# Turned down product, first layer's second norm on VectorE, and layer two's first weights asked for after the gathers

## The reference

```python
def moe(x, w_router, router_bias, w_gate, w_up, w_down):
    t = x.reshape(B * S, D)                     # D = 1024
    combine = route(t, w_router, router_bias)   # two experts per token, weighted
    h = silu(einsum('td,edf->tef', t, w_gate)) * einsum('td,edf->tef', t, w_up)   # f = 512
    y = einsum('tef,efd->td', h * combine[:, :, None], w_down)

for i in range(DEPTH):                          # 2 layers
    mix = attention(x) if i % 2 == 0 else pool_mix(x)
    x = layer_norm(ALPHA * x + mix, ln1_g[i], ln1_b[i])
    x = layer_norm(ALPHA * x + moe(x, ...), ln2_g[i], ln2_b[i])
```

## Time and profile before

| | |
|---|---|
| median of 3 runs | 1211.73 us (1211.29 to 1215.57) |
| profiled execution, its own time | 1213.42 us |
| its span | 1211.7 us |
| mean granted TensorE clock | 0.932 |
| PE busy | 1054.5 us (87%) |
| DVE busy | 370.1 us (31%) |
| ACT busy | 194.0 us (16%) |
| POOL busy | 111.2 us (9%) |
| DMA | 296.04 MB, mean 244 GB/s |
| chain that ended last | PE 83%, DVE 7%, DMA 4% |

### The profile page before, as it was taken

How to read it: one execution, slowest core, us unless ns; L and a number is a source line. 1 busy time by engine, 2 the same in 40 slices (tenths; PEclk the granted TensorE clock), 3 DMA queues, 4 the chain that set the end, 5 groups by cost and what they waited for, 6 DMA issues and landing times.

```text
span 1211.7 us, 28356 instructions
## 1 busy us (share of the span) xinstructions
PE 1054.5 (87%) x11923; PEld 740.8 (61%) x11923; DVE 370.1 (31%) x798; ACT 194.0 (16%) x428; POOL 111.2 (9%) x184
## 2 busy tenths in 40 slices
PE   7899999899899932999999999178189999999985
PEld 6677777544444322677677668067067776776752
DVE  1334444322433251111111111497511111111117
ACT  1234444400222112000000000131020000000000
POOL 0001001030033103000000000321300000000012
PEclk9999999899999965999999999677589999999997
DMA  9324335230023097999999999606359999999915
GB/s 342 146 86 133 106 112 178 82 79 1 1 78 92 26 392 274 350 384 392 395 385 394 397 389 392 215 3 246 141 200 387 386 395 391 387 400 389 377 51 201
DMA packets 80864, 296.04 MB, mean 244 GB/s; under 512 B 10184, under 2 KB 41168, under 8 KB 72495
## 3 DMA queue, kind: packets, MB, share of 16 engines
q1 hardware_dynamic: 53351, 247.50, 54.5%
q10 hardware_dynamic: 19712, 26.75, 6.5%
q0 software_dynamic: 7760, 21.24, 5.1%
HBM read 255.80 MB, written 40.11 MB: 244 GB/s over the span
## 4 chain that ended last, share of the span: by engine, by line
PE 83%; DVE 7%; DMA 4%; POOL 2%; issue 2%; ACT 2%; ACTq 0%; SPq 0%; POOLq 0%; DVEq 0%
PE PS L896 19%; PE PS L874 15%; PE PS L884 14%; PE PS L801 5%; PE PS L573 4%; PE PS L738 4%; PE PS L620 3%; PE PS L636 3%; PE PS L761 2%; PE PS L529 2%; PE PS L629 2%; PE PS L719 2%; PE PS L551 2%; POOL expert_rows L1036 2%; PE PS L806 1%
## 5 line engine op out<-in xcount | busy, mean ns | idle before, releaser
L896 PE MATMUL PS<-ring,arena 128*96 128x512 f32 x512 | 227.4, 597 | 0.0
L874 PE MATMUL PS<-arena,ring 128*64 128x96 f32 x4096 | 180.5, 250 | 53.5 <-DVE arena L1649 53.5
L874 PEld LDWEIGHTS PS<-arena,ring 128*64 128x64 f32 x4096 | 174.4, 140 | 77.4 <-issue 77.4
L884 PE MATMUL PS<-arena,ring 128*64 128x96 f32 x4096 | 174.4, 246 | 0.0
L884 PEld LDWEIGHTS PS<-arena,ring 128*64 128x64 f32 x4096 | 170.9, 137 | 0.0
L896 PEld LDWEIGHTS PS<-ring,arena 128*96 128x96 f32 x512 | 80.8, 163 | 123.0 <-issue 119.2
L1649 DVE STREAM_TRANSPOSE arena<-arena 128x768 uint32<-128x768 uint32 x34 | 54.2, 1593 | 206.7 <-ACT arena L1227 176.6
L1669 DVE COPY arena<-PS 96x512 f32<-96x512 f32 x32 | 22.0, 687 | 218.0 <-PE PS L896 218.0
L1231 ACT ACTIVATE arena<-PS 96x512 f32<-96x512 f32 x32 | 19.0, 593 | 379.3 <-PE PS L896 379.3
L801 PE MATMUL PS<-ring,arena 128*128 128x512 f32 x128 | 55.7, 594 | 0.7 <-issue 0.7
L1002 POOL DMA_DIRECT2D ring<-cache_krope x64 | 34.6, 541 | 141.3 <-issue 141.3
(11 more groups left out here) (245 smaller groups left out, 1061.2 us busy)
## 6 DMA issues: line engine op xcount, KB each, us to landing
ring<-w_gate SPq DMA_DIRECT2D x32, 2048.0 KB, 15.2
ring<-w_up SPq DMA_DIRECT2D x32, 2048.0 KB, 15.9
ring<-w_down SPq DMA_DIRECT2D x32, 2048.0 KB, 16.3
arena<-expert_rows ACTq DMA_DIRECT2D x144, 96.0 KB, 9.6
expert_out<-arena ACTq DMA_DIRECT2D x32, 384.0 KB, 8.3
expert_rows<-ring SPq DMA_DIRECT2D x6, 1920.0 KB, 10.1
ring<-cache_ckv SPq DMA_DIRECT2D x64, 128.0 KB, 2.1
ring<-w_o SPq DMA_DIRECT2D x1, 4096.0 KB, 19.3
```

The lines of the kernel that those rows point to most:

```text
L874: last = nc.tensor.matmul(bank(s, KF, CAP)[at:at + 64, f, :], wg[w][:, k, P * f + at:P * f + at + 64], xeT[s][:, k, :], start=(k == 0), st ...
L884: last = nc.tensor.matmul(out[at:at + 64, :], wu[w][:, k, P * f + at:P * f + at + 64], xeT[s][:, k, :], start=(k == 0), stop=(k == KD - 1))
L896: last = nc.tensor.matmul(bank(4 + hf)[0:CAP, :], h[s][:, f, :], wd[w][:, f, 512 * hf:512 * (hf + 1)], start=(f == 0), stop=(f == KF - 1))
```

## The change

The down product is turned: w_down becomes the stationary side in chunks of 64 columns and `h` streams, as in gate and up. Its result comes out transposed (`yT`, features on the partitions). ACT and DVE copy the two halves of `yT` out of PSUM, and PE transposes it back (`turn_back`) after the first quarter of the next tile's gate product. Then the rows are copied and stored, one tile later than before. The last tile's is turned back behind the loop.

The second norm of layer one is done by DVE alone, with the sequence of the first norm (`norm`); ACT gives only the deviation. GpSimd issues the gathers alone.

SP asks for `pool_scale` and `state_pool` first, waits for all five gathers, and then asks for layer two's first expert.

```diff
@@ SP
-                    load_expert(1, 0, 1, (S[0]["gate_ps"][0], nh), (S[0]["up_ps"][0], 2 * nh), (S[0]["down_ps"][0], nh))
-
                     sp.wait_ge(S[0]["xeT_set"], 2 * nh + 1)
                     sp.wait_ge(S[0]["xe_ld"][1], 64 * (nh + 1))
                     sp.dma_start(pscale, bcast(t["pool_scale"][0])).then_inc(st_ld, 16)
                     sp.dma_start(state[0:DB * CTX, :], t["state_pool"][0].rearrange("b c d -> (b c) d")).then_inc(st_ld, 16)
 
+                    for slot, rows in ((0, 64), (1, 64), (2, 32)):
+                        sp.wait_ge(gath[slot], rows)
+                    load_expert(1, 0, 1, (S[0]["gate_ps"][0], nh), (S[0]["up_ps"][0], 2 * nh), (S[0]["down_ps"][0], 2 * nh))
+
                     sp.wait_ge(ln_out[0], 2 * NT)
@@ PE, experts
+                def turn_back(tl):
+
+                    pe.wait_ge(q["yT_set"], 2 * tl + 2)
+                    for m in range(KD):
+                        last = nc.tensor.transpose(bank(4 + m // 4, 4, P)[0:CAP, m % 4, :], yT[:, m, :], ident)
+                    last.then_inc(q["back_ps"], 1)
+
                 def tile(u, s):
...
                     for f in range(KF):
+                        if f == 1:
+                            turn_back(tl)
                         for k in range(KD):
...
-                    for blocks in (range(KF - 1), (KF - 1,)):
-                        if KF - 1 in blocks:
-                            pe.wait_ge(q["h_set"], 2 * tl + 2)
-                        for hf in range(2):
-                            for f in blocks:
-                                last = nc.tensor.matmul(bank(4 + hf)[0:CAP, :], h[s][:, f, :], wd[w][:, f, 512 * hf:512 * (hf + 1)],
+
+                    def down(m, blocks):
+                        for f in blocks:
+                            for at in (0, 64):
+                                last = nc.tensor.matmul(bank(4 + m // 4, 4, CAP)[at:at + 64, m % 4, :],
+                                                        wd[w][:, f, P * m + at:P * m + at + 64], h[s][:, f, :],
                                                         start=(f == 0), stop=(f == KF - 1))
-                    last.then_inc(q["down_ps"][s], 1)
+                        return last
+
+                    down(0, range(KF - 1))
+                    down(4, range(KF - 1))
+                    pe.wait_ge(q["h_set"], 2 * tl + 2)
+                    down(0, (KF - 1,))
+                    down(4, (KF - 1,))
+                    for m in (1, 2, 3, 5, 6, 7):
+                        last = down(m, range(KF))
+                        if m in (3, 7):
+                            last.then_inc(q["down_ps"][s], 1)
@@ ACT, experts
+                def store(tl, s, count):
+
+                    act.wait_ge(q["back_ps"], tl + 2)
+                    act.wait_ge(q["y_st"][s], count)
                     nc.scalar.activation(ys[s][0:CAP, 0:512], bank(4)[0:CAP, :], ACT.Copy).then_inc(q["y_set"], 1)
                     act.wait_ge(q["y_set"], 2 * tl + 4)
                     act.dma_start(yd[bass.ds(CAP * tl, CAP), :], ys[s][0:CAP, :]).then_inc(q["y_st"][s], 16)
 
+                def tile(u, s, more):
+                    tl = 2 * u + s
+
+
+                    act.wait_ge(q["xeT_set"], tl + 1)
+                    load_rows(s, bass.ds(CAP * (tl + 2), CAP))
+                    if more:
+                        store(tl - 1, 1 - s, 16 * (u + s))
+                    act.wait_ge(q["gate_ps"][s], u + 1)
+                    nc.scalar.activation(sg[s], bank(s, KF, CAP), ACT.Silu).then_inc(q["sg_set"], 1)
+                    act.wait_ge(q["down_ps"][s], 2 * u + 1)
+                    nc.scalar.activation(yT[:, 0:4, :], bank(4, 4, CAP), ACT.Copy).then_inc(q["yT_set"], 1)
@@ DVE, experts
+                def rows_back(tl, s, count):
+                    dve.wait_ge(q["back_ps"], tl + 2)
+                    dve.wait_ge(q["y_st"][s], count)
+                    v.tensor_copy(ys[s][0:CAP, 512:D], bank(5)[0:CAP, :]).then_inc(q["y_set"], 1)
...
-                    v.tensor_copy(ys[s][0:CAP, 512:D], bank(5)[0:CAP, :]).then_inc(q["y_set"], 1)
+                    dve.wait_ge(q["down_ps"][s], 2 * u + 2)
+                    v.tensor_copy(yT[:, 4:8, :], bank(5, 4, CAP)).then_inc(q["yT_set"], 1)
@@ ACT, between the layers
-                    normalise(0, step)
+                    deviation(0, 1, step)
@@ DVE, between the layers
                 if step < NT:
-                    stats(0, 1, step)
-                if 2 <= step <= NT:
-                    gain(0, step - 1)
-                if step < NT:
-                    spread(0, step)
-                if step == 0:
-                    gain(0, 0)
+                    norm(0, 1, step)
@@ POOL, between the layers
                 gather(3)
-                for i in range(NT):
+                if L == 0:
+                    gather(4)
+                for i in range(NT if L else 0):
                     shift(L, i)
```

More of the change, by code:

```diff
@@ L338, in expert_sems @@
             two = ("wg_ld", "wu_ld", "wd_ld", "xe_ld", "y_st", "gate_ps", "up_ps", "down_ps")
-            one = ("xeT_set", "sg_set", "h_set", "y_set")
+            one = ("xeT_set", "sg_set", "h_set", "yT_set", "back_ps", "y_set")
             return {n: [sem(f"{n}{s}_{L}") for s in range(2)] for n in two} | {n: sem(f"{n}_{L}") for n in one}
@@ L904, in experts @@
                         tile(u, s)
+                turn_back(2 * nh)
             pe.wait_ge(wo_ld, 16)
@@ L1211, in experts @@
                 act.sem_inc(q["y_set"], 1)
+                for s in range(2):
+                    act.sem_inc(q["y_st"][s], 16)
                 act.wait_ge(scat, 160 * (L + 1))
@@ L1218, in experts @@
                     nc.scalar.activation(X[0:n, i, :], X[0:n, i, :], ACT.Copy, scale=ALPHA).then_inc(xscaled, 1)
-                def tile(u, s, stored):
+                def store(tl, s, count):
+                    act.wait_ge(q["back_ps"], tl + 2)
+                    act.wait_ge(q["y_st"][s], count)
+                    nc.scalar.activation(ys[s][0:CAP, 0:512], bank(4)[0:CAP, :], ACT.Copy).then_inc(q["y_set"], 1)
+                    act.wait_ge(q["y_set"], 2 * tl + 4)
+                    act.dma_start(yd[bass.ds(CAP * tl, CAP), :], ys[s][0:CAP, :]).then_inc(q["y_st"][s], 16)
+                def tile(u, s, more):
                     tl = 2 * u + s
@@ L1239, in experts @@
                     tile(u, 1, True)
+                store(2 * nh - 1, 1, 16 * nh)
             def take_pages(b):
@@ L1503, in stats, with norm @@
                 v.bn_aggr(mv[0:n, i, :], bn[0:n, i, :]).then_inc(ln_agg, 1)
-            def norm1(L, i):
-                n = rows_of(i)
-                x, gains, offsets = X[0:n, i, :], gb[0:n, 0, :], gb[0:n, 1, :]
-                stats(L, 0, i)
+            def norm(L, which, i):
+                n, k = rows_of(i), NT * which + i + 1
+                x, gains, offsets = X[0:n, i, :], gb[0:n, 2 * which, :], gb[0:n, 2 * which + 1, :]
+                stats(L, which, i)
                 if i == 0:
-                    dve.wait_ge(gb_ld[L][0], 32)
-                dve.wait_ge(ln_agg, 2 * NT * L + i + 1)
+                    dve.wait_ge(gb_ld[L][which], 32)
+                dve.wait_ge(ln_agg, 2 * NT * L + k)
                 link(v.scalar_tensor_tensor(out=x, in0=x, scalar=mv[0:n, i, 0:1], in1=gains, op0=ALU.subtract, op1=ALU.mult))
-                dve.wait_ge(ln_std, 2 * NT * L + i + 1)
+                dve.wait_ge(ln_std, 2 * NT * L + k)
                 link(v.reciprocal(rstd[0:n, i:i + 1], std[0:n, i:i + 1]))
@@ L1646, in experts @@
                 dve.sem_inc(q["y_set"], 1)
+                dve.sem_inc(q["yT_set"], 2)
                 def turn_rows(s):
@@ L1654, in experts, with tile @@
                 turn_rows(0)
-                def tile(u, s, stored):
+                def rows_back(tl, s, count):
+                    dve.wait_ge(q["back_ps"], tl + 2)
+                    dve.wait_ge(q["y_st"][s], count)
+                    v.tensor_copy(ys[s][0:CAP, 512:D], bank(5)[0:CAP, :]).then_inc(q["y_set"], 1)
+                def tile(u, s, more):
                     tl = 2 * u + s
+                    if more:
+                        rows_back(tl - 1, 1 - s, 16 * (u + s))
                     dve.wait_ge(q["sg_set"], tl + 1)
@@ L1679, in _ @@
             for i in range(4):
-                norm1(0, i)
+                norm(0, 0, i)
             samples()
-            norm1(0, 4)
+            norm(0, 0, 4)
             route(0)
@@ L1705, in _ @@
                         dve.wait_ge(pool_out, 32)
-                    norm1(1, step - 4)
+                    norm(1, 0, step - 4)
             route(1)
```

27 lines of the change are left out of this document (10 added, 17 removed).

## The result

The changed kernel takes 1197.34 us (median; 1193.22 to 1199.47) against 1213.47 (1211.29 to 1215.57) for the kernel before in the same comparison: a ratio of 0.9856 [0.9813, 0.9899]. One of its four executions took 1441.04 us at a mean granted clock of 0.726 (the others 1193.22, 1195.20 and 1199.47) and is left out of the range and of the ratio; the median takes it in and would be 1195.20 without it. The profiled execution took 1199.47 us, 13.95 less than the 1213.42 before. Faster, as forecast, and inside the stated range, but by about half of the 31.9 us of the sum (16.1 by the medians, 17.5 by the ratio, 13.95 by the profiled executions), and outside the likeliest case's own range of 1174 to 1190.

A forecast was written before the change was run, and what follows sets the result against it. TensorE was taken to set the pace of the expert loops, with weight transfers close behind. Loops -25.6, loop ends +3.2, store landing -2.0 and between layers -7.5 made -31.9 us from 1213.42: 1181 us, range 1174 to 1204.

The forecast's parts named there:

- the 31.9 us of the sum: Whole kernel: loops -25.6, loop ends +3.2, store landing -2.0, between the layers -7.5, together -31.9 us.
- the likeliest case: Whole kernel: the forecast of 1181 us holds, with a range of its own of 1174 to 1190; chance 0.67.
- Gate ... now follows a 64-column one: -0.15: Expert tile: gate loses the cost of following a product with another array shape, -0.15 us per tile.
- twice the switch: Expert tile: bound with two shape switches and transposes 0.02 us slower each, leaving a gain of -0.6 us per tile.
- 16 x 0.90 ... -13.4: Each expert loop: TensorE alone would give 14.4 us, less about 1 for the slow first tile, so -13.4.
- rival A: Expert loops: TensorE's longer body is no longer kept and is refetched each turn; 1223 to over 1350 us; chance 0.12.
- The bytes are unchanged, so the last w_down of the loop still lands near 744 us: Layer one's loop: down of the last tile ends no earlier than 749.5 against 762.27, so -12.8 us per layer.
- to near 27: Expert loops, sign: w_down landings grow about 1.1 us per tile, from 14, perhaps with a short wait at the end.
- Rival B: Expert loops: a tile takes 17.3 us, giving 1195, or the weights' queue falls 5 us further behind, 1191; chance 0.16.
- VectorE no longer stands before the fourth tile: Layer two's first norm: no wait for TensorE's pooling product, so the last norm ends at 838.9 instead of 844.05, -5.1 us.
- With TensorE waiting for VectorE some 3 to 4 are left: Router's end in layer two: its 6.7 us behind the last norm shrink to 3 to 4.
- Rival C: Each expert tile: the copy of yT comes late and TensorE's stall takes up the 0.9 us; 1204 to 1213; chance 0.05.

The follow-up runs named there:

- e5_light: Changed kernel with only two of four w_down blocks loaded inside the loops (stale weights in the rest): 1188.49 us, loops 279.2 and 276.8.
- e8_first_light: Changed kernel with a quarter of the weight blocks loaded during each loop's first turn: 1189.34 us, second tile 17.0 us in both loops.
- e9_fast: Changed kernel with one of eight transposes and six of eight down chunks per tile, so TensorE runs ahead: 1189.2 us, loops 276.9 and 275.4.
- e10_few_rows: The kernel of e9_fast with each tile's row loads in the loop cut to four small pieces (stale rows): 1128.14 us.
- e3_order: Kernel before, with only the request for layer two's first weights moved behind the gathers: ratio 0.9977 [0.9956, 0.9998].
- e2_norm: Kernel before, with only the second norm moved to VectorE alone: ratio 0.9961 [0.9941, 0.9981].
- e0_after: The changed kernel measured again without edit, against the kernel before: 1196.5 us against 1213.9, ratio 0.9849 [0.9816, 0.9881].
- e7_rows_first: Complete changed kernel with ScalarE's copy of the third tile's transposed rows put ahead of the fifth tile's deviation: 1190.15 us, ratio 0.9814 to the kernel before.
- e6_one_back: Changed kernel with one of the eight transposes per tile kept: 1191.27 us, loops 278.4 and 279.3.

## Why the forecast was right and wrong

**The tile: nearly right.** 17.00 instead of 16.85. Down (-1.76), the transposes (0.11 each) and the copy of yT (0.56, hidden) were as priced. The step that failed is "Gate ... now follows a 64-column one: -0.15", read without what the transposes do to it: they have the full array's shape, so there is a switch into them as well as out of them. The sum counts one; the second stands only in the bounds ("twice the switch"), and the measured -0.75 lies inside their -1.2 to -0.6. 0.15 x 16 is 2.4 us a loop.

**TensorE's limit of a loop: 4.0 us too low.** "16 x 0.90 ... -13.4" gives 272.5 us for layer one; e5_light needed 276.5. The difference is the 2.4 us above and 2.5 of the second tile there (19.54 instead of 17.00), less about 1.0 in the first tile, 18.92 where the forecast's allowance makes it 19.8 and the second switch 19.9.

**The code: rival A falls, its neighbour came.** In layer one no block is fetched after the first turn, in a body of 1,568 records; in layer two a single one comes, in the third turn, and no tile of the middle shows a stop. That agrees with 2,048 instructions in the Trainium skill (Runtime: NRT & Kernel Launch, Instruction fetch mechanics) and not with its rule of a two-page window at a taken branch. The queue was priced as if only a refetch could meet it ("in the full DMA queue it could stand as long as a weight request"). The first fetch meets it too: 2.1 and 1.4 us in all, in the first turn alone, gone in e8_first_light. Before, that tile shows no stall (17.75).

**The transfers' limit: the step that failed most.** "The bytes are unchanged, so the last w_down of the loop still lands near 744 us", which is 268.0 us after the loop's start. It landed 272.0 after it, and down ended 5.6 later, at 277.6: the whole length of the loop, to a tenth. The bytes are indeed the same; the rate is not. The last 13 steps of the queue took 240.0 us instead of 234.4. Of these 5.6 us, 5.3 lie in the five long steps while the landings passed from 18 to 28 us, which the loop before never reached (17.5 at its last), and 0.5 in the request that the stopped second tile made late; the first landing came 1.5 sooner after the loop's start. That long steps come with such landings at whatever place of the loop, e9_fast shows, and that they need the row loads, e10_few_rows; how the one makes the other stays open. The forecast saw landings growing "to near 27" and priced them as free. Rival B named this size in its second sentence, "falling behind by some 5 us more than the floor has it would give the same (1191)", at 0.16 with its TensorE half; that is the case that came. Its two halves came together, and as they bound the same end they cost 4.5 and 5.4 us a loop and not their sum. In sum the loops gave 8.3 and 7.4 us instead of 12.8 each, 9.9 missing.

**Ends of the loops: right.** The store is issued 2.7 us after down's end instead of 0.9 (+1.8, forecast 1.6), and layer two's end is 1.4 longer. The landing went from 5.07 to 3.05, -2.0 as forecast, and e3_order gives it alone, as far as the landing goes; the gather behind it took another 0.5 less. No stall for the first weights shows.

**Between the layers: VectorE right in one execution of two, the router's end wrong.** From the first weighed addition to the end of the last norm 62.8 us, the number of the forecast, in steps of 6.92 (forecast 6.94) and 5.54. (The forecast's own sum says -5.1 for it; its 67.8 less 62.8 is 5.0.) "VectorE no longer stands before the fourth tile" holds there, and in e2_norm, but not in e0_after, the same kernel: 1.91 us of wait at TensorE's lower clock, and 64.8 us. The forecast had the clock of that stretch in no term. "With TensorE waiting for VectorE some 3 to 4 are left" of 6.7 us failed: they stayed, because TensorE waited for ScalarE, and ScalarE, in its order, for the fifth tile's statistics before it copied the third tile's rows (the row of 832.84, idle 4.72). e7_rows_first changes that order alone and gets 4.35 us. The forecast had followed VectorE and TensorE, and left ScalarE's queue out.

**Rival C** didn't come: the transposes follow gate's first quarter with no idle time in the chain.

**Sum.** 9.9 us are missing in the loops and 2.3 between them, 12.2; the remaining 5.6 of the profiled execution's shortfall is the later start of its first loop, which e0_after doesn't have. The range held because B's case was in it, at 0.16: right by a rival, and not by the case given 0.67, which was too much for a floor read off unchanged bytes.

**Left open.** Which packets the row loads' meet when steps become long, and whether larger pieces for the rows would free their 2.0 us: not tried, it needs another layout of the gathered rows.

## What to carry to other kernels

When TensorE becomes faster over a transfer queue that already falls behind, take the queue's pace from its worst stretch, not from its mean: here how late it ran was part of its speed, and loads that were 6% of the bytes were 11% of its time. Count a change of array shape once into and once out of every interleaved group, and look for the first fetch of a longer loop body behind the loop's own transfers. When a stall should vanish, follow every engine's own order up to it: the next to be late is often an instruction queued behind one that waits for something unrelated.

## What the runs showed of the hardware

- Switching between a product on 64-column tiles and full-width transposes cost 0.15 us each way at a granted clock of 1.00: 1.01 us for eight transposes and 0.25 for one (e6_one_back), so 0.11 each and 0.14 besides, and 4.11 for the 96 records behind them, worth 3.96.
- A loop body of 1,568 TensorE records was kept from turn to turn (no code packet from 520 to 750 us, one from 920 to 1150); its first fetch stalled the engine 1.4 to 2.5 us in all behind 2 MB transfers (two executions of the changed kernel, two loops each) and not at all behind loads of a quarter of that (e8_first_light).
- 0.4 MB of row loads in 1 KB pieces cost 2.0 us of DMA time beside 6.3 MB of weights: 394 GB/s at steps of 18.0 with them, 422 at steps of 16.0 without. The step from one 2 MB landing to the next went from 18.0 to as much as 20.0 us while landings grew from 18 to 28 us (394 GB/s before, 378 in that stretch), and back to 17.9 above that, with the DMA share at 1.02 all the time.
